# Sums of squares of twelve head pairs as two rounded products each, in a one-core trunk layer

## The reference

```
h    = rmsnorm(x) ;  p = h @ w_in          # 2048 x 5376 columns, split into xa ga bg cg xb q k v
q, k = rmsnorm per head of 128 values      # 6 heads each
ya   = rg_lru(conv4(xa)) * gelu(ga)        # 6 heads
yb   = bg * conv3(cg * xb)                 # 4 heads
yc   = stick-breaking attention(q, k, v)   # 6 heads
y    = rmsnorm per head of 128 values of [ya, yb, yc], times mix_norm
x    = x + y @ w_out
x    = x + two of 32 experts per token (w_gate, w_up, w_down of each expert, 12 MB together)
```

## Time and profile before

| | us |
|---|---|
| median of 3 runs | 1313.36 |
| lowest, highest | 1310.47, 1313.62 |
| the profiled execution, its own time | 1310.38 |
| its span (first to last instruction) | 1308.6 |
| PE busy in the span | 1129.7 |
| DVE busy, ACT busy | 510.0, 280.5 |
| 16 DMA queues, share of the span | 88% |

### The profile page before, as it was taken

How to read it: one execution, slowest core, us unless ns; L and a number is a source line. 1 busy time by engine, 2 the same in 40 slices (tenths; PEclk the granted TensorE clock), 3 DMA queues, 4 the chain that set the end, 5 groups by cost and what they waited for, 6 DMA issues and landing times.

```text
span 1308.6 us, 17772 instructions
## 1 busy us (share of the span) xinstructions
PE 1129.7 (86%) x7343; PEld 658.1 (50%) x7343; DVE 510.0 (39%) x817; ACT 280.5 (21%) x444; POOL 57.3 (4%) x72
## 2 busy tenths in 40 slices
PE   8999999999999988878787887987887797779677
PEld 7888888878885444324323323423242253234223
DVE  6646677775444353223222222322232232222223
ACT  7445576684430000000000000000000000000000
POOL 3000011501100000000000000000000000000000
PEclk9999999999999888888878978888788798888888
DMA  9955554746678999999999999999999999999996
GB/s 323 293 190 176 159 181 140 246 129 201 273 297 336 425 435 429 430 432 430 432 433 432 432 431 430 433 433 433 432 432 433 431 431 433 433 433 430 431 424 262
DMA packets 83856, 471.61 MB, mean 360 GB/s; under 512 B 7154, under 2 KB 68192, under 8 KB 69216
## 3 DMA queue, kind: packets, MB, share of 16 engines
q1 hardware_dynamic: 83808, 470.94, 88.2%
HBM read 468.83 MB, written 2.10 MB: 360 GB/s over the span
## 4 chain that ended last, share of the span: by engine, by line
PE 52%; DMA 40%; DVE 4%; ACT 1%; issue 1%; POOL 1%; DVEq 0%; SPq 0%; ACTq 0%
PE banks L1465 16%; DMA twin<-in_w_gate 15%; DMA twin<-in_w_up 15%; DMA twin<-in_w_down 10%; PE banks L1697 9%; PE banks L1467 8%; PE banks L1743 6%; PE banks L1677 3%; PE banks L1647 3%; PE banks L1663 3%; DVE x_acc L1337 2%; PE banks L1407 1%; PE banks L1486 1%; DVE up_sb L1350 1%; POOL h_tok L555 1%
## 5 line engine op out<-in xcount | busy, mean ns | idle before, releaser
L1697 PE MATMUL banks<-twin,x_exp 128*32 128x512 f32 x1760 | 252.5, 698 | 83.2 <-DMA twin<-in_w_gate 68.0
L1337 DVE TENSOR_TENSOR x_acc<-x_acc,banks 128x512 f32<-128x512 f32 x256 | 158.5, 682 | 343.5 <-PE banks L1647 343.4
L1465 PE MATMUL banks<-hT,w_split 128*128 128x512 f32 x576 | 203.9, 398 | 0.1
L989 DVE TENSOR_TENSOR w_split<-ring,w_split 128x1024 fp32r<-128x1024 f32 x116 | 146.7, 1284 | 112.6 <-ACT w_split L676 112.0
L1697 PEld LDWEIGHTS banks<-twin,x_exp 128*32 128x32 f32 x1760 | 50.0, 118 | 236.2 <-issue 131.7
L1467 PE MATMUL banks<-hT,w_split 128*128 128x256 f32 x576 | 161.2, 280 | 0.0
L1743 PE MATMUL banks<-twin,hidT 128*32 128x512 f32 x864 | 144.3, 829 | 19.3 <-DVE hidT L1356 9.7
L676 ACT ACTIVATE w_split<-ring 128x1024 fp32r<-128x1024 f32 x116 | 121.7, 1060 | 122.0 <-PE banks L1467 121.9
L1465 PEld LDWEIGHTS banks<-hT,w_split 128*128 128x128 f32 x576 | 108.0, 188 | 25.4 <-issue 0.3
L888 ACT ACTIVATE y_item<-banks 64x512 f32<-64x512 f32 x32 | 18.9, 591 | 472.4 <-PE banks L1743 472.4
L1467 PEld LDWEIGHTS banks<-hT,w_split 128*128 128x128 f32 x576 | 108.7, 189 | 0.2
(11 more groups left out here) (244 smaller groups left out, 925.9 us busy)
## 6 DMA issues: line engine op xcount, KB each, us to landing
twin<-in_w_gate SPq DMA_DIRECT2D x28, 4096.0 KB, 32.5
twin<-in_w_up SPq DMA_DIRECT2D x27, 4096.0 KB, 32.3
twin<-in_w_down SPq DMA_DIRECT2D x27, 4096.0 KB, 32.3
ring<-in_w_in SPq DMA_DIRECT2D x20, 2048.0 KB, 9.0
ring<-in_w_up SPq DMA_DIRECT2D x10, 2048.0 KB, 15.8
ring<-in_w_down SPq DMA_DIRECT2D x10, 2048.0 KB, 16.7
ring<-in_w_out SPq DMA_DIRECT2D x8, 2048.0 KB, 8.3
ring<-in_w_gate SPq DMA_DIRECT2D x7, 2048.0 KB, 11.8
```

The costliest lines, as they stand in the source:

```text
L989: dve.tensor_tensor(w_lo[:, k], src, w_hi[:, k].bitcast(F32), ALU.subtract).then_inc(lo_ready, 1)
L1337: dve.tensor_tensor(dst, dst, b_comb[n][:, :], ALU.add).then_inc(acc_done, 1)
L1465: pe.matmul(dst[:, 0:2 * PW], stationary[:, 0, cols], moving.rearrange("p s n -> p (s n)"), start=(k == 0 and cc == 0), stop=False)
L1697: ins = pe.matmul(dst[SLOTS * j:SLOTS * (j + 1), :], x_exp[:, c, cols], weights[:, cc * F:(cc + 1) * F], start=(c < 4), stop=(c >= KC - 4))
```

## The change

It does four things. (1) For the six q and k pairs, the three yc pairs and the three ya pairs, ACT makes a rounded (fp32r) high part of the squares: `ACT.Square` of the values themselves for q and k (one pair at each n from 2 to 7), `ACT.Copy` of POOL's squares for y (three pairs at n = 18, three at n = 19). (2) DVE subtracts it from POOL's squares and rounds the rest, at the same n, behind `add_projection`. (3) PE sums both parts with rounded ones in two fp32r products of 512 columns (`split_sums`) in place of the fp32 ones. (4) `yb_sums(0)` stands ahead of quarter 2 of piece 20 instead of quarter 1, and on ACT the Ln of that pair stands behind `y_split_high(0)` and the Exp of the ya pairs.

```diff
--- before.py
+++ after.py
@@ -139,13 +139,20 @@
         lru_w = at("lru_w", [2, HA, P], F32, o + BLK_BG * SEQ * 4)
         lru_a = at("lru_a", [HA, SEQ], F32, o + BLK_BG * SEQ * 4)
         scores2 = at("scores2", [2, 2, TILES * P + P], F32, o + BLK_K * SEQ * 4)
+        hi_k = at("hi_k", [HC, SEQ], F32R, o + (BLK_BG + HA) * SEQ * 4)
+        lo_c = at("lo_c", [HC, SEQ], F32R, o + BLK_K * SEQ * 4)
+        lo_a = at("lo_a", [HA, SEQ], F32R, o + BLK_XA * SEQ * 4)
         o += BLK_V * SEQ * 4
+        hi_q = at("hi_q", [HC, SEQ], F32R, o)
         v_tok = at("v_tok", [TILES, HC * P], F32, o)
         o += TILES * HC * P * 4
         temp = at("temp", [12, SEQ], F32, o)
         gain_rows = at("gain_rows", [P], F32, o)
         scores0 = at("scores0", [2, 2, TILES * P + P], F32, o)
         scores1 = at("scores1", [2, 2, TILES * P + P], F32, o + 6 * SEQ * 4)
+        hi_c = at("hi_c", [HC, SEQ], F32R, o)
+        hi_a = at("hi_a", [HA, SEQ], F32R, o + 6 * SEQ * 4)
+        qk_lo = at("qk_lo", [2 * HC, SEQ], F32R, o)
         x2T = at("x2T", [2, 2, SEQ], F32, o + 6 * SEQ * 4)
         cross = at("cross", [NX + QI, NE], F32, o + 6 * SEQ * 4)
         match = at("match", [NX + QI, NE], F32, o + 6 * SEQ * 4 + (NX + QI) * NE * 4)
@@ -184,6 +191,8 @@
         table_scratch = at("table_scratch", [8], F32, o + 2688 + 2112)
         give0 = at("give0", [TILES, P], F32, o + 2688 + 2144)
         assert base + o + 2688 + 2144 + 1024 <= 229344
+        ones_r = at("ones_r", [P], F32R, o + 2688 + 2144 + 1024)
+        assert base + o + 2688 + 2144 + 1024 + 512 <= 229344
         y_item, give = [y_item0, y_item1], [give0, give1]
         scores = [scores0, scores1, scores2]
 
@@ -237,6 +246,7 @@
         hT_hi_ready, hT_ready = sem("hT_hi_ready"), sem("hT_ready")
         lam_exp = sem("lam_exp")
         qk_sq, qk_ready = sem("qk_sq"), sem("qk_ready")
+        qk_high, qk_low, y_high, y_low = sem("qk_high"), sem("qk_low"), sem("y_high"), sem("y_low")
         conv_ready = sem("conv_ready")
         z_masked, ln_ready = sem("z_masked"), sem("ln_ready")
         logw_ready, w_ready = sem("logw_ready"), sem("w_ready")
@@ -378,6 +388,19 @@
 
         Y_RUNS = {3: [(3, 12, 16)], 0: [(5, 0, 4)], 1: [(7, 4, 8)], 2: [(3, 10, 12), (8, 8, 10)]}
 
+        def qk_high_part(j):
+            return (hi_q, hi_k)[2 * j // HC][:, 2 * j % HC:2 * j % HC + 2, :]
+
+        def y_high_part(j):
+            return (hi_c, hi_a)[2 * j // HC][:, 2 * j % HC:2 * j % HC + 2, :]
+
+        def y_low_part(j):
+            return (lo_c, lo_a)[2 * j // HC][:, 2 * j % HC:2 * j % HC + 2, :]
+
+        def y_squares(j):
+            b = BLK_K + 2 * j if j < HC // 2 else BLK_XA + 2 * j - HC
+            return proj[:, b:b + 2, :]
+
         block = ctx.enter_context(nc.Block())
 
 
@@ -680,6 +703,18 @@
                 act.wait_ge(quarter_used, 4 * n + 4)
                 act.activation(proj_place(n), cross_part(n), ACT.Copy).then_inc(cross_out, 1)
 
+            def qk_squares_high(j):
+
+                act.wait_ge(proj_free, j + 1)
+                act.activation(qk_high_part(j), proj[:, BLK_Q + 2 * j:BLK_Q + 2 * j + 2, :],
+                               ACT.Square).then_inc(qk_high, 1)
+
+            def y_squares_high(pairs):
+
+                for j in pairs:
+                    act.wait_ge(y_sq, j + 1)
+                    act.activation(y_high_part(j), y_squares(j), ACT.Copy).then_inc(y_high, 1)
+
             def stick_scores(b):
 
                 z = scores[b][:, 0]
@@ -791,6 +826,12 @@
                 if n == 1:
                     parameters()
                     load_table(ACT.Ln)
+                if 2 <= n < HC + 2:
+                    qk_squares_high(n - 2)
+                if n == 18:
+                    y_squares_high(range(0, HC // 2))
+                if n == 19:
+                    y_squares_high(range(HC // 2, (HC + HA) // 2))
                 if n == 6:
                     norm_log(range(U_QK, U_QK + 4), temp)
                 if n == 8:
@@ -834,9 +875,9 @@
                 if n == 20:
                     norm_log(range(U_YA, U_YB), rstd_a)
                     split_high(N_IN, range(0, 1))
-                    norm_log(range(U_YB, U_YB + 1), rstd_b)
                     y_split_high(0)
                     norm_exp(range(U_YA, U_YB), rstd_a)
+                    norm_log(range(U_YB, U_YB + 1), rstd_b)
                     norm_exp(range(U_YB, U_YB + 1), rstd_b)
                 if n == N_IN:
                     load_table(ACT.Ln)
@@ -993,6 +1034,20 @@
                 dve.wait_ge(cross_out, n + 1)
                 dve.tensor_tensor(proj_place(n), proj_place(n), main_part(n), ALU.add).then_inc(proj_free, 1)
 
+            def qk_squares_low(j):
+
+                dve.wait_ge(qk_sq, j + 1)
+                dve.wait_ge(qk_high, j + 1)
+                sq = temp[:, 2 * j:2 * j + 2, :]
+                dve.tensor_tensor(qk_lo[:, 2 * j:2 * j + 2, :], sq, qk_high_part(j).bitcast(F32), ALU.subtract).then_inc(qk_low, 1)
+
+            def y_squares_low(pairs):
+
+                for j in pairs:
+                    dve.wait_ge(y_high, j + 1)
+                    dve.tensor_tensor(y_low_part(j), y_squares(j), y_high_part(j).bitcast(F32),
+                                      ALU.subtract).then_inc(y_low, 1)
+
             def normalise_qk(pairs):
                 for j in pairs:
                     dve.wait_ge(rstd_ready, j + 1)
@@ -1092,6 +1147,14 @@
                     split_low(n)
                     if n < N_IN:
                         add_projection(n - 1)
+                if n == 1:
+                    dve.tensor_copy(ones_r[:, :], ones[:, :])
+                if 2 <= n < HC + 2:
+                    qk_squares_low(n - 2)
+                if n == 18:
+                    y_squares_low(range(0, HC // 2))
+                if n == 19:
+                    y_squares_low(range(HC // 2, (HC + HA) // 2))
                 if n == 2:
                     softplus_lam()
                 if n == 8:
@@ -1446,7 +1509,7 @@
                     if isinstance(n, int) and n == 0:
 
                         pe.wait_ge(hT_ready, 2 * k + 2)
-                    if isinstance(n, int) and n == N_IN - 1 and k == 1:
+                    if isinstance(n, int) and n == N_IN - 1 and k == 2:
 
                         yb_sums(0)
                     if isinstance(n, int) and n == N_IN:
@@ -1486,6 +1549,13 @@
                     ins = pe.matmul(use(u)[:, b * SEQ:(b + 1) * SEQ], ones[:, :], squares[:, b, :], start=True, stop=True)
                 ins.then_inc(aux_full, 1)
 
+            def split_sums(u, high, low):
+
+                dst = use(u)
+                pe.matmul(dst[:, :], ones_r[:, :], high.rearrange("p b n -> p (b n)"), start=True, stop=False)
+                pe.matmul(dst[:, :], ones_r[:, :], low.rearrange("p b n -> p (b n)"),
+                          start=False, stop=True).then_inc(aux_full, 1)
+
             def yb_sums(j):
                 pe.wait_ge(y_sq, (HC + HA) // 2 + j + 1)
                 sums(U_YB + j, proj[:, BLK_CG + 2 * j:BLK_CG + 2 * j + 2, :])
@@ -1497,8 +1567,8 @@
             piece(1, 1, "w")
             def qk_sums(pairs):
                 for j in pairs:
-                    pe.wait_ge(qk_sq, j + 1)
-                    sums(U_QK + j, temp[:, 2 * j:2 * j + 2, :])
+                    pe.wait_ge(qk_low, j + 1)
+                    split_sums(U_QK + j, qk_high_part(j), qk_lo[:, 2 * j:2 * j + 2, :])
 
             def stick_scores(b):
 
@@ -1559,12 +1629,12 @@
                 ins.then_inc(aux_full, 1)
             pieces(17, 19, "w")
             for j in range(HC // 2):
-                pe.wait_ge(y_sq, j + 1)
-                sums(U_YC + j, proj[:, BLK_K + 2 * j:BLK_K + 2 * j + 2, :])
+                pe.wait_ge(y_low, j + 1)
+                split_sums(U_YC + j, y_high_part(j), y_low_part(j))
             piece(19, 1, "w")
             for j in range(HA // 2):
-                pe.wait_ge(y_sq, HC // 2 + j + 1)
-                sums(U_YA + j, proj[:, BLK_XA + 2 * j:BLK_XA + 2 * j + 2, :])
+                pe.wait_ge(y_low, HC // 2 + j + 1)
+                split_sums(U_YA + j, y_high_part(HC // 2 + j), y_low_part(HC // 2 + j))
             piece(20, 0, "w")
 
             logits_bank = bank[AUX + 2]
```

## The result

| | before | after |
|---|---|---|
| median of 20 runs, us | 1311.33 | 1314.69 |
| lowest to highest, us | 1309.20 to 1314.09 | 1311.36 to 1317.10 |
| profiled execution, span, us | 1308.6 | 1314.5 |

The changed kernel is slower by a ratio of 1.0020 (95% interval 1.0013 to 1.0026), 2.6 us of 1311.3 (1.7 to 3.4). Beside later runs of the kernel before it came out at 1.002 again (12 runs, 1.001 to 1.003). More runs of the kernel before brought its median down from 1313.36 to 1311.33.

What follows compares the result with a forecast made beforehand. PE bounds the mixer stage, except near piece 20, where ACT and DVE set the end. `yb_sums(1)` 3.55 us later, less 2.3 for q and k, plus 1.15 for clock: 1313.36 + 2.4 = 1315.8 us, range 1309.5 to 1318.0.

Steps and rivals of the forecast that it cites:

- the rival with the clock: After piece 21's long gap PE's clock stays half twice as long as at 384 us; +4.1 us, 1317.5; chance 0.10.
- the sum: `yb_sums(1)` 3.55 us later, less 2.3 for q and k, gives +1.24; with 1.15 for clock, +2.4 us.
- Part 1: PE's fp32r products save 0.383 us a pair, 4.6 us in all, 5.2 at most, only where PE comes last.
- Part 2: Added ACT and DVE work costs nothing, except three DVE subtractions at n = 19, 1.9 us later for the convolution.
- The slip: At n = 19, DVE's subtractions beside POOL's product start the convolution 1.9 us later; bounds 0 to 1.9.
- Part 3: ACT at n = 20: two more loads and the moved Ln stretch 4.55 us to 7.68; the tail keeps 7.95.
- Part 4: `yb_sums(0)` a quarter later on PE costs nothing; POOL's squares come about 1.5 us after the old place would ask.
- The clock: Behind piece 21's 7.8 us wait, 3.4 us at half clock loses 1.7 us; 0.55 goes into quarter 3's wait, +1.15.
- the saving that arrives whole: Rival: PE's wait at 283.93 doesn't grow, as ACT and DVE have slack; -4.6 us, 1308.8; chance 0.12.
- main case: Longer ACT chain at n = 20, PE's wait of 7.8 us and lost clock: +2.4 us, 1315.8; chance 0.58.

Runs made afterwards that it cites:

- re-ordered version: Changed kernel's products, without the extra loads, all parts at n = 18, what `yb_sums(1)` waits for put first at n = 21; ratio 0.9972 to kernel before, median 1307.87 us.

## Why the prediction was right, point by point

The forecast was +2.4 us, to be told from nothing by less than 0.3%; measured +2.6 (1.7 to 3.4), and within 0.3%. The absolute time, 1315.8, was 1.1 too high, as the median of three that it was added to was 2.0 above that of 20. The mechanism was the one argued: a longer chain on ACT, a longer wait of PE, and clock lost by it. That the number fits so closely is partly luck. Several terms were off in size, and the profiled mixer stages moved by +3.9 and +3.5 us, nearer to the rival with the clock than to the sum's +2.4.

- **Part 1.** 0.46 us a pair, so 0.40 saved and not 0.383: 4.8 us in all. Of q and k's share 1.0 us was given back by the slower pitch, which I hadn't foreseen. The -2.3 us in the sum should have been -1.38.
- **Part 2.** Nothing seen at n = 2 to 7, as said (the run with q and k alone). The Square brought no table load: in the changed kernel's trace the first one starts at 40.73 us, before the copy that stands ahead of it (40.26 us, 0.58 long) is quite done. At n = 19 the two engines held each other up: the convolution started no earlier than in the kernel before (256.03 against 255.99) though the piece ended 1.38 us sooner. The slip is therefore 1.4 us and not 1.9, and `normalise_y` of yc moved by 266.47 + 1.38 - 268.02 = -0.17 us on the old clock, not by +0.42.
- **Part 3.** 8.00 us, forecast at 7.68; the tail 277.80 to 285.73 = 7.93, forecast at 7.95. The two loads are shown by the run that takes them back: 2.9 us of wait, 2.2 us of time. The Trainium skill, "ScalarE: Activation LUTs", section "Table sets: the hidden batching unit", has one set for both functions. That did not hold for this program: Ln behind Exp and Exp behind Ln each have a load in the rows above. The drain that its section "What ACT_TABLE_LOAD costs" adds to a load didn't appear either: from the load at 270.88 to the start of the Exp at 272.18 it is 1.30 us.
- **Part 4.** Neutral as long as the long wait stands behind it, as the run with the old place shows: 1.94 us of new wait, forecast at 1.5, and the second sum 0.1 us from its time.
- **The sum.** `yb_sums(1)` came at 285.73, +1.80 us against +1.24; the wait was 7.69 at 7.8.
- **The clock.** The term with the worst size. 5.7 us at half clock behind the wait, not 3.4, so 2.85 us of work lost, not 1.7. Less the 0.55 us ahead of quarter 3 that is +2.3, where I had +1.15; the profiled mixer stage's end moved by +3.9 in all, of which +1.80 is the sum's, so +2.1 came of it. The timed runs moved by 2.6. What makes the 1.3 between isn't shown. The runs with q and k alone and with 30 idle products show that the clock can fall behind a wait of 2 us too, so the kernel before may lose some of it in some executions; how often wasn't measured. In the second profile of the changed kernel the mixer stage moved by 3.5, so part of it is scatter.

Of the rivals, the saving that arrives whole is not what the re-ordered version gives: of its 3.7 us about 2.8 are the products', of 4.8 saved by the distances on PE. Another 1.0 went into the slower pitch. So the saving was real, and most of it had only its way blocked. The slower case by the clock stood at +4.1 us with 6.8 us at half; the trace came to 5.7, nearer to it than to the main case.

## What to carry to other kernels

An engine that is busy all the time is still not what sets the end at the few places where the chain of waits leaves it: before cheapening its work, look at who hands it the next thing there and what stands ahead of that in the other engine's list. On ACT count changes of function, not instructions: moving one Ln behind the Exps, with the first gated sum a quarter later, cost 4.3 us here (two loads, the Ln itself in the chain, and the clock lost by the longer wait), about what twelve cheaper pairs of sums can save (4.8 us on PE). And when a saving vanishes, first put what the late step waits for at the head of its queue.

## What the runs showed of the hardware that I had not expected

- PE has two pitches at the same granted clock of 1.00. The pair of a 512- and a 256-column product repeats after 0.347 or 0.353 us, pieces take 11.09 or 11.31 us, and it changes at the groups of sums: in every profile but one it goes to the slower one at the four pairs after piece 5, fp32 or rounded, and behind the two pairs after piece 7 it is the faster again where they are fp32, and not where they are rounded. The one exception, the kernel with only q and k rounded, was 0.2 us a piece slower from piece 1 on. The cause is open.
- A POOL product and DVE's subtractions beside it hardly overlapped: of three subtractions that need 0.69 us each, one took 2.89, beside a POOL product that went from 2.40 to 2.78. Together they took 4.0 us (252.02 to 256.03), where alone it is 1.9 and 2.40.
- Behind a wait of about 2 us the clock stayed up in the profile of the kernel before (1.97 us) and in that with the first gated sum back at quarter 1 (1.94 us), and fell for some 3 us in those of the kernels with q and k alone and with 30 idle products. Ahead of the second gated-convolution sum it stayed up behind every wait of 1.4 to 1.6 us, and fell with every wait of 4.8 to 7.7 us. With idle products placed at the start of the long wait it stayed up.
